# Attention weights turned unnormalised by PE transposes, the result divided afterwards

## The reference

```python
scores = jnp.where(valid, scores + bias, -jnp.inf)
m = jnp.maximum(jnp.max(scores, axis=-1, keepdims=True), sink_b)
p = jnp.exp(scores - m)
denom = jnp.sum(p, axis=-1, keepdims=True) + jnp.exp(sink_b - m)
o = jnp.einsum("bnkgqs,bnskd->bnqkgd", (p / denom), vb)
```

## Time and profile before

| what | us |
|---|---|
| median of 3 runs | 1866.28 (1865.23 to 1866.74) |
| the profiled execution | 1863.45 |
| its span in the trace | 1861.6 |
| PE busy | 1810.2 (97% of the span) |
| POOL, DVE, ACT busy | 1106.6, 912.2, 757.9 |

### The profile page before, as it was taken

The page is one execution under the profiler, slowest core; times in us unless marked ns, Lnnn a source line. Parts: engine busy times, 40 slices in busy tenths (PEclk is TensorE's granted clock), DMA queues, the critical chain, the costliest instruction groups (busy, mean ns, idle before and its releaser), DMA issues.

```text
span 1861.6 us, 24985 instructions
## 1 busy us (share of the span) xinstructions
PE 1810.2 (97%) x8168; PEld 1489.5 (80%) x8168; DVE 912.2 (49%) x1193; ACT 757.9 (41%) x998; POOL 1106.6 (59%) x589
## 2 busy tenths in 40 slices
PE   5999999999899999999999999999999999999996
PEld 4888888888678888888888888888877888888885
DVE  7644442269846444432255444323897554544223
ACT  2433332246865333332333333223578543333221
POOL 3544457769767444457744444666886844444674
PEclk9999999999999999999999999999999999999998
DMA  4332223331012322223332322333211233232331
GB/s 147 113 101 94 96 74 97 109 103 63 24 62 98 101 93 98 92 78 94 118 107 91 101 90 86 85 95 121 68 46 46 80 102 101 90 101 72 92 101 52
DMA packets 53435, 166.84 MB, mean 90 GB/s; under 512 B 6000, under 2 KB 6256, under 8 KB 53360
## 3 DMA queue, kind: packets, MB, share of 16 engines
q1 hardware_dynamic: 52128, 163.78, 27.6%
q10 hardware_dynamic: 1232, 2.10, 0.3%
HBM read 163.76 MB, written 2.10 MB: 89 GB/s over the span
## 4 chain that ended last, share of the span: by engine, by line
PE 90%; issue 4%; POOL 3%; DVE 3%; DMA 0%; ACT 0%; DVEq 0%; POOLq 0%; ACTq 0%
PE bank L1167 29%; PE bank L1168 29%; PE bank L1169 29%; POOL y_conv L450 1%; PE bank L1312 1%; POOL x L510 1%; POOL diag L459 1%; POOL w_lo L399 1%; DVE xs_hi L855 1%; PE bank L1299 0%; DVE xs_lo L783 0%; PE bank L1185 0%; DVE bank L945 0%; DMA x<-xT 0%; DVE den L983 0%
## 5 line engine op out<-in xcount | busy, mean ns | idle before, releaser
L399 POOL TENSOR_TENSOR w_lo<-stage,w_hi 128x1024 fp32r<-128x1024 f32 x352 | 872.2, 2479 | 663.9 <-ACT w_hi L530 663.8
L530 ACT ACTIVATE w_hi<-stage 128x1024 fp32r<-128x1024 f32 x352 | 372.8, 1060 | 885.6 <-PE bank L1169 881.9
L1167 PE MATMUL bank<-xs_hi,w_hi 128*128 128x512 f32 (+1 forms) x1712 | 667.6, 390 | 19.0 <-DVE xs_lo L783 18.9
L1168 PE MATMUL bank<-xs_lo,w_hi 128*128 128x512 f32 (+1 forms) x1712 | 663.5, 388 | 0.0
L1169 PE MATMUL bank<-xs_hi,w_lo 128*128 128x512 f32 (+1 forms) x1712 | 663.4, 388 | 0.0
L1167 PEld LDWEIGHTS bank<-xs_hi,w_hi 128*128 128x128 f32 x1712 | 322.1, 188 | 87.1 <-DVE xs_lo L783 18.9
L1168 PEld LDWEIGHTS bank<-xs_lo,w_hi 128*128 128x128 f32 x1712 | 322.0, 188 | 67.1 <-issue 1.9
L1169 PEld LDWEIGHTS bank<-xs_hi,w_lo 128*128 128x128 f32 x1712 | 321.9, 188 | 65.4
L810 DVE TENSOR_TENSOR work<-bank,rstd 128x512 f32<-128x512 f32 x176 | 120.7, 690 | 401.1 <-PE bank L1169 400.2
L1167 PE MATMUL bank<-h_hi,w_hi 128*128 128x512 f32 x704 | 273.9, 389 | 0.0
L1168 PE MATMUL bank<-h_lo,w_hi 128*128 128x512 f32 x704 | 273.9, 389 | 0.0
(11 more groups left out here) (137 smaller groups left out, 1298.8 us busy)
## 6 DMA issues: line engine op xcount, KB each, us to landing
stage<-w_gu SPq DMA_DIRECT2D x176, 512.0 KB, 3.3
stage<-w_down SPq DMA_DIRECT2D x64, 384.0 KB, 3.1
stage<-w_down SPq DMA_DIRECT2D x64, 320.0 KB, 2.9
stage<-w_in SPq DMA_DIRECT2D x24, 512.0 KB, 3.3
stage<-w_out SPq DMA_DIRECT2D x16, 512.0 KB, 3.4
x<-xT ACTq DMA_DIRECT2D x4, 512.0 KB, 6.6
stage<-w_in SPq DMA_DIRECT2D x8, 256.0 KB, 2.7
out<-result SPq DMA_DIRECT2D x8, 256.0 KB, 2.2
```

The lines of the kernel that those rows point to most:

```text
L399: nc.gpsimd.tensor_tensor(w_lo[:, r, :], stage[:, r, :], w_hi[:, r, :].bitcast(F32), ALU.subtract).then_inc(split, 1)
L530: nc.scalar.activation(w_hi[:, r, :], stage[:, r, :], ACT.Copy).then_inc(hi_made, 1)
L1167: nc.tensor.matmul(to, wh, mh, start=first, stop=False)
L1168: nc.tensor.matmul(to, wh, ml, start=False, stop=False)
```

## The change

PE now turns the bare exponentials with the identity as a transpose, so that no turning waits for a denominator and `diag` is gone. The values get a layout of their own, `v[:, block, key head, 128]`, padded with zeros for the other key head (two memsets on DVE before the mixing step, two copies on ACT instead of one), so that both key heads of a query block add up in one bank: `weigh_values` of the first key head opens the sum, that of the second closes it. The division comes afterwards, once per query block: the eight reciprocals of a token are widened to 64 columns each (`widen`, POOL), turned by four multiplications with the identity (`spread_denominators`, PE), copied to SBUF (`keep_factors`, ACT) and multiplied into the result (`normalise`, DVE), which takes the place of ACT's `evict_o`. The small sums go from DVE to POOL and are made per query block on 128x8 elements (`sink_args`, `denominators`); only the reciprocal stays on DVE. Where each step stands is set by tables: at which unit, or in which round of POOL's loop over groups.

The core of the diff (waits and shapes as they are, index arithmetic cut):

```diff
+SINK_AT = [1, 9, 17, 23]
+DEN_IN = [1, 3, 5, 6]
+WIDEN_IN = [2, 4, 6, 7]
+RECIP_AT = [6, 14, 22, 27]
+SPREAD_AT = [9, 17, 25, 29]
+KEEP_AT = [10, 18, 26, 30]
+EVICT_AT = [11, 19, 27, 32]
...
-                def diagonals(g):
-                    pool.wait_ge(r_den_made, l * N_GROUPS + g + 1)
...
+                def sink_args(b):
+                    pool.wait_ge(scores_taken, l * N_UNITS + (b + 1) * 2 * GROUP)
+                    nc.gpsimd.tensor_tensor(sink_arg[...], neg_max[...], par[...], ALU.add).then_inc(sink_ready, 1)
+                def denominators(b):
+                    pool.wait_ge(sink_exped, l * NB + b + 1)
+                    pool.wait_ge(exped, l * N_UNITS + (b + 1) * 2 * GROUP)
+                    nc.gpsimd.tensor_tensor(den[...], p_sum[...], sink_exp[...], ALU.add).then_inc(den_made, 1)
+                def widen(b):
+                    pool.wait_ge(r_den_made, l * NB + b + 1)
+                    if b:
+                        pool.wait_ge(factors_spread, l * NB + b)
+                    for kv in range(N_KV_HEADS):
+                        nc.gpsimd.tensor_tensor(r_wide[:, :, kv, :],
+                                                r_den[:, 2 * b + kv, :].unsqueeze(2).to_broadcast([P, GROUP, HEAD_DIM]),
+                                                zero[:, 0:1].unsqueeze(2).to_broadcast([P, GROUP, HEAD_DIM]),
+                                                ALU.add).then_inc(r_widened, 1)
...
-                for g in range(N_GROUPS - 1):
-                    late = 2 if done < NC * P_TAPS else 0
+                for g in range(N_GROUPS):
+                    if g % 2 and g < N_GROUPS - 1:
+                        sink_args(g // 2 + 1)
+                    if g in DEN_IN:
+                        denominators(DEN_IN.index(g))
+                    if g in WIDEN_IN:
+                        widen(WIDEN_IN.index(g))
+                    late = 4 if done < NC * P_TAPS else 0
                     add_products(done, late)
-                    diagonals(g + 1)
-                    add_products(done + late, late)
...
+                def keep_factors(b):
+                    act.wait_ge(factors_spread, l * NB + b + 1)
+                    if b:
+                        act.wait_ge(o_evicted, l * NB + b)
+                    nc.scalar.activation(token_factors[:], att_bank("spread", b, 0)[:], ACT.Copy).then_inc(factors_kept, 1)
...
+                def normalise(b):
+                    dve.wait_ge(o_made, l * N_GROUPS + 2 * b + 2)
+                    dve.wait_ge(factors_kept, l * NB + b + 1)
+                    nc.vector.tensor_tensor(y_attn[:, :, b * P:(b + 1) * P],
+                                            side_bank[:].rearrange("p (c q) -> p c q", q=P),
+                                            token_factors[:].rearrange("p (c q) -> p c q", q=P),
+                                            ALU.mult).then_inc(o_evicted, 1)
...
                     pe.wait_ge(exped, l * N_UNITS + g * GROUP + c + 1)
-                    pe.wait_ge(diag_made, l * N_UNITS + g * GROUP + c + 1)
                     bank_taken(k)
                     for i in range(n):
-                        last = nc.tensor.matmul(att_bank("turned", g, c)[:, i * P:(i + 1) * P],
-                                                probs[g % PROBS][:, c, i * P:(i + 1) * P], diag[:, c, :],
-                                                start=True, stop=True)
+                        last = nc.tensor.transpose(att_bank("turned", g, c)[:, i * P:(i + 1) * P],
+                                                   probs[g % PROBS][:, c, i * P:(i + 1) * P], ident[:])
...
+                    if b and not kv:
+                        pe.wait_ge(o_evicted, l * NB + b)
                     for i in range(n):
-                        last = nc.tensor.matmul(side_bank[:], v[:, first + i, :],
-                                                pt[:, g % 2, i, :, :].rearrange("p c q -> p (c q)"), start=i == 0,
-                                                stop=i == n - 1)
+                        last = nc.tensor.matmul(side_bank[:], v[:, first + i, kv, :],
+                                                pt[:, g % 2, i, :, :].rearrange("p c q -> p (c q)"),
+                                                start=not kv and i == 0, stop=bool(kv) and i == n - 1)
...
+                def spread_denominators(b):
+                    pe.wait_ge(r_widened, (l * NB + b + 1) * N_KV_HEADS)
+                    bank_taken(ATT["spread", b, 0])
+                    for c in range(GROUP):
+                        last = nc.tensor.matmul(att_bank("spread", b, 0)[:, c * P:(c + 1) * P],
+                                                r_wide[:, c, :, :].rearrange("p h d -> p (h d)"),
+                                                ident[:], start=True, stop=True)
+                    last.then_inc(factors_spread, 1)
```

More of the change, by code:

```diff
@@ L106, in attention_turns @@
             turns.append(("scores", *UNITS[u + LEAD]))
+        if u in SPREAD_AT:
+            turns.append(("spread", SPREAD_AT.index(u), 0))
     return {turn: n for n, turn in enumerate(turns)}
@@ L660, in _ @@
                 exp_scores(0, 3)
-                exp_sink(0)
                 exp_scores(1, 0)
@@ L667, in _ @@
                 exp_scores(1, 3)
-                exp_sink(1)
                 act.wait_ge(v_turned, l + 1)
-                nc.scalar.activation(v[:].rearrange("p b d -> p (b d)"), side_bank[:], ACT.Copy).then_inc(v_made, 1)
+                for kv in range(N_KV_HEADS):
+                    at = slice(HEAD_DIM * kv, HEAD_DIM * (kv + 1))
+                    nc.scalar.activation(v[:, :, kv, at], side_bank[:].rearrange("p (b d) -> p b d", d=P)[:, :, at],
+                                         ACT.Copy).then_inc(v_made, 1)
                 for c in range(3):
@@ L694, in _ @@
                         done += 1
-                    if c == GROUP - 1 and g:
-                        evict_o(g - 1)
+                    if u in SINK_AT:
+                        exp_sink(SINK_AT.index(u))
+                    if u in KEEP_AT:
+                        keep_factors(KEEP_AT.index(u))
                     if 20 <= u < 24:
@@ L1066, in _ @@
                             merge(2)
-                        if (u + LEAD) % GROUP == GROUP - 1:
-                            sink_args((u + LEAD) // GROUP)
-                    if c == 0 and g + 1 < N_GROUPS:
-                        denominators(g + 1)
+                    if u in RECIP_AT:
+                        reciprocals(RECIP_AT.index(u))
+                    if u in EVICT_AT:
+                        normalise(EVICT_AT.index(u))
                     if u == len(LATE_TAPS):
```

102 lines of the change are left out of this document (45 added, 57 removed).

## The result

The changed kernel takes 1867.9 us (median of 20 runs, 1866.0 to 1874.9); the kernel before, on the same chip, 1865.2 us (20 runs, 1863.3 to 1866.9). The ratio is 1.0024, 95% interval 1.0014 to 1.0034: slower by 0.14 to 0.34%, 2.6 to 6.3 us; the two medians by themselves differ by 2.7 us, 0.14%.

The account below looks back on a forecast made before the run. PE, busy 97% of the span, bounds the kernel; DVE paces the attention's first stretch. Per layer -1.0 schedule and +2.5 clock, two layers +3.0, less 0.2: +2.8 us on 1866.28, so 1869; own range 1864 to 1874, with rivals 1857 to 1880.

Parts of the forecast that it names:

- The savings: Attention, per layer: DVE net about -6 us in the first stretch, PE net -5.2 and -2.6 us in the two stretches.
- (b): POOL's first widening stands behind adding unit 7's product and a channel addition: done at 482.2, PE can spread at 482.5.
- (c): PE reaches the first spread after scores 21, at 477.7, and stands there 4.8 us.
- Step (d): After the first spread DVE is the chain: second reciprocal 493.6, spread 495.4, channel sum 499.7 instead of 500.68.
- Step (e): Second stretch: third spread waits 3.1 us for POOL's widening; projection at 519.6 instead of 520.59, layer 1.0 us faster.
- The clock: Behind each of the two waits, one 3.3 us stretch at 1.2 GHz, 1.25 us each: +2.5 us per layer.
- (1): Rival: waits at the spreads are short, POOL widening earlier or other engines not running dry; 1857 us, chance 0.25.
- (2): Rival: short transposes make the clock fall again and again, half the attention at 1.2 GHz; 1880 us, chance 0.20.
- (3): Rival: the same schedule at full clock; 1864.3 us, chance 0.10.

Follow-up runs that it names:

- pool_early: Changed kernel with only POOL's list altered, the widenings of the first and third query blocks placed earlier; 1860.12 us, ratio 0.9974 to the kernel before.
- all_moves: pool_early plus second widening before POOL's weight slot, last two weight slots after fourth widening, later sum of convolution's squares, ACT's first copy one step earlier; 1846.16 us.
- warm: Changed kernel with PE doing 14 and 11 unused identity multiplications in the waits before the first and third spread; 1865.49 us, ratio 1.0000 to the kernel before.
- warm_both: warm with six more unused identity multiplications in the wait before the sum of the convolution's squares; 1863.10 us, ratio 0.9985 to the kernel before.
- by_identity: Changed kernel with its 80 transposes per layer made as multiplications with the identity; 1874.90 us, ratio 1.0047 to the kernel before.
- sums_dve: pool_early with the small sums back on DVE, still once per query block; 1865.24 us, ratio 0.9995 to the kernel before.

## Why the prediction was right

**The savings held.** A block of the turning costs 0.08 us (476.11 to 476.35 for three; 0.09 predicted), a spread 0.99 in pool_early (0.94), two widenings 1.15 (1.35), a small sum on POOL 0.16 (0.13). DVE lost 5.6 us of busy time in the first stretch (6). PE's busy time fell by less than reckoned: at full clock (all_moves) 31.07 to 27.68, -3.4 instead of -5.2. Each burst of records ends with a modelled tail, and shorter bursts with more gaps have more of them; that this is the whole difference was not tested.

**Steps (b) and (c): the first wait.** Widened at 482.2 predicted, 482.24 by the start of the next instruction, spread at 482.40 (482.5), wait 4.15 us (4.8): PE came there at 478.25 instead of 477.7. DVE idle beside it for 5.47 us, as expected. pool_early shows the cause: with two products fewer and no channel addition ahead of the widening the wait is gone.

**Step (d)** is judged on warm, at full clock, since in the changed kernel's profile the low clock moves all of it (spread 497.91, channel sum 502.17): second reciprocal 493.34 (493.6), spread 495.48 (495.4), channel sum 499.74 (499.7).

**Step (e):** third wait 3.17 us (3.1). In warm that spread is at 509.67 (509.1) and the projection at 520.07 (519.6), in a layer that started 0.2 us earlier than before's; so the layer is some 0.3 us faster, not 1.0; the second layer gives the same (55.65 us from unit 0's turning to the projection in warm, 55.98 before). The 2.0 us that the sum credited to the schedule are 0.3 to 0.6.

**The clock: the right cause, an uneven size.** One stretch of 3.3 us behind each of the two waits, 1.25 us each, 5.0 in all, was predicted. In the profile the stretches are 6.9 us behind the first wait in both layers and 6.4 behind the third, the latter only in the second layer; and there are two more, of 3.5 us, behind a wait of 1.3 us at the convolution's statistic, which the profiled execution of before has too, with no fall. That is 27 us at 1.2 GHz in an execution with a mean clock of 0.988. In the eleven runs at 0.992 to 0.994 it must be far less: a mean clock that is 0.006 higher over 1872 us, at half the clock, means by estimate 22 us less at 1.2 GHz for those at 0.994. So the same program, with the same waits by its lists, loses its clock behind most of them in one run and behind few in the next. Measured as the distance from warm_both the loss is 7.3 us on average.

**The total came out right partly by luck.** The forecast added the difference of -2.0 + 5.0 - 0.2 us to the median of 1866.28, on the premise that the 2.8 us between before's profiled execution and its median carry over unchanged. They don't: they are low clock that most runs of before have and the profiled one hasn't (see warm_both), and the changed kernel's waits bring a loss of their own. From full clock the forecast amounts to a schedule 2.0 us faster and 7.8 us of low clock (2.8 + 5.0); the runs show a schedule 0.3 us faster and 7.3 us. Beside before it is +2.8 predicted and +4.5 (2.6 to 6.3) by the ratio, +2.7 by the medians. The schedule was credited with 1.7 us too much, and that is as large as the gap to +4.5. The lower end of the range, 1864, takes nothing off for errors in the hops, though the upper end adds them; the result doesn't touch it.

**The rivals.** (1) needed short waits at the spreads; they were long, and its time of 1857 is near what pool_early reached once they were gone (1860.1). (2) said that the low clock comes from the short transposes. It fell behind waits, with transposes or with multiplications (by_identity), and not in the attentions of pool_early, warm_both or all_moves, which keep every transpose; and at the convolution's statistic it falls although PE turns nothing there. By the Trainium skill, "TensorE: Matmul & The Clock Gate", in its part on the PE-mode transpose, they do not count as PE work for the clock in the same way; no run here shows a fall that needs this rule. The prediction applied it too strictly: besides the spread and the values the scores are multiplications too, and would hold the clock up by the same rule. (3), full clock, is the kernel warm_both, in which PE does extra work to keep it: 1863.10, 1.2 us under its 1864.3.

What stays open: why the clock fell at some waits of 1.3 to 3.2 us and not at others of the same length. The third wait kept its clock in the first layer and lost it in the second; the statistic's wait is the same 1.3 us in before and after; and where before's runs at 0.992 to 0.994 lose their clock no trace shows, since only one at 0.995 was profiled.

## What to carry to other kernels

Work taken off the engine that paces a stretch pays only when nothing in the new order makes the matrix engine stand: put the short instruction on which it waits directly behind its own input in the helper's list, not behind products that come later. Price a wait of the matrix engine at its length plus half of the stretch at the lower clock that may follow, and count the old waits as well as the new. Before adding a difference read in one profiled execution to a median, compare the granted clock of that execution with that of the other runs. And before judging such a change by its total, run it once with the waits filled and once with them removed; here the same change measured +0.24%, -0.15% and, with the lists put in order, -1.05%, of which -0.29% can be had without the change.

## What the runs showed of the hardware

**Filling a wait keeps the clock.** 28 records of multiplications whose result nobody reads, in the 4.15 us ahead of the first spread, kept the granted clock at 1.00 behind it in both layers and made the eight records of the spread 1.16 us long instead of 2.07. With all three waits of a layer filled, the range of the runs fell from 8.9 us (20 runs of the changed kernel) to 1.1 (11 runs), and none of the 11 had a mean clock under 0.995.

**POOL's elementwise work holds some of DVE's.** In pool_early a sum of squares of 128x512 on DVE, two operands in SBUF, takes 0.69 us alone and 2.65 and 2.89 beside a slot of weights that takes POOL 2.35 us; without the slots all three take 0.69. In sums_dve the additions of 128x512 on POOL hold sums of 8 elements for up to 1.17 us in the same way. The taps, of which one operand is in PSUM, keep their 0.75 us (22 of them in the first stretch, 749 ns on average, beside a POOL that is busy for 25.4 of 32.6 us). The Trainium skill, "SBUF — State Buffer", section "SBUF: two separate sides", says that GpSimd and a DVE operation with two SBUF inputs take a shared pair of ports in turn, each for a whole instruction; the rows agree. It fits this that the change made DVE 5.6 us less busy by moving sums of a few elements.
